# Modulation chunks two slots earlier, the norms in four banks and the first batch's solution ahead of the second's level, in a hybrid delta-rule, state-space and mixture-of-experts layer

## What is computed

```
mod = silu(c) @ w_ada + b_ada            # 6 x 1024 shifts, scales and gates
u   = modulate(x, shift1, scale1) @ w_in  # and the same for the context
q, k, v, xs, b, c = silu(dwconv(u))       # 5 taps along the tokens
k = l2norm(k); q = l2norm(q) / 8          # over 64 channels of each head
M = I + tril(beta k k^T * exp(G_i - G_j)) # per chunk of 64 tokens, head, direction
U = M^-1 (beta v);  W = M^-1 (beta k exp(G))
S = S exp(g_last) + k_dec^T (U - W S)     # chunk after chunk: 4 of the context, 4 of the tokens
o = q exp(G) S + (q k^T * decay) v_new    # two directions, then norm and gate
x = x + g1 * rms_norm(concat(o, ssd) @ w_out)
x = x + g2 * rms_norm(moe(modulate(x, shift2, scale2)))   # 32 experts, 4 per token
```

## Time and profile before

| | |
|---|---|
| median of three timed runs | 1428.35 us (1425.06 to 1429.14) |
| the profiled execution's own time | 1420.88 us |
| its span, first to last instruction | 1419.1 us |
| mean granted TensorE clock | 0.956 |
| TensorE busy | 1255.7 us (88%) |
| VectorE busy | 485.3 us (34%) |
| ScalarE busy | 254.8 us (18%) |
| GpSimd busy | 122.0 us (9%) |

### The profile page before, as it was taken

One profiled execution on the slowest core, in us unless ns is written; L12 is line 12 of the kernel. 1 busy time (PEld: TensorE's weight loads), 2 busy tenths in 40 slices (PEclk: granted clock), 3 DMA queues, 4 the chain that ended last, 5 costly groups with the idle time before them and its releaser, 6 DMA issues.

```text
span 1419.1 us, 25289 instructions
## 1 busy us (share of the span) xinstructions
PE 1255.7 (88%) x10245; PEld 570.7 (40%) x10246; DVE 485.3 (34%) x1026; ACT 254.8 (18%) x494; POOL 122.0 (9%) x169
## 2 busy tenths in 40 slices
PE   5999898547897999999898988987999999999995
PEld 2645354446744333333333333332333333333432
DVE  1255359815767322221222212221222212212223
ACT  2321532325223111111111111110000100100101
POOL 0200370163401000000000000000000000000000
PEclk9999999657997999999999999999999999999998
DMA  9929210000384999999999999999999699969993
GB/s 356 357 88 370 87 55 35 4 33 4 136 297 189 426 425 428 428 426 426 428 427 428 426 426 427 427 426 424 428 427 428 260 426 427 427 265 429 427 427 146
DMA packets 48134, 458.59 MB, mean 323 GB/s; under 512 B 4416, under 2 KB 4816, under 8 KB 22736
## 3 DMA queue, kind: packets, MB, share of 16 engines
q1 hardware_dynamic: 48080, 457.81, 77.8%
HBM read 456.15 MB, written 1.05 MB: 322 GB/s over the span
## 4 chain that ended last, share of the span: by engine, by line
PE 57%; DMA 29%; DVE 6%; issue 3%; ACT 2%; POOL 1%; DVEq 0%; SPq 0%; ACTq 0%; POOLq 0%
DMA arena<-in_w_up 29%; PE bank L1155 22%; PE bank L1184 8%; PE bank L667 7%; PE bank L1126 3%; PE bank L1117 2%; PE bank L1048 2%; PE bank L583 2%; PE bank L543 2%; DVE arena L1727 1%; ACT arena L1542 1%; PE bank L592 1%; DMA arena<-in_x 1%; PE bank L1148 1%; PE bank L897 1%
## 5 line engine op out<-in xcount | busy, mean ns | idle before, releaser
L1155 PE MATMUL bank<-arena 128*64 128x512 f32 x2176 | 482.8, 596 | 35.2 <-DMA arena<-in_w_up 19.5
L1155 PEld LDWEIGHTS bank<-arena 128*64 128x64 f32 x2176 | 154.1, 137 | 345.2 <-issue 269.4
L1184 PE MATMUL bank<-arena 128*64 128x512 f32 x1088 | 239.3, 592 | 0.0
L2254 DVE TENSOR_SCALAR arena<-bank 128x512 f32<-128x512 f32 x34 | 23.6, 693 | 394.0 <-PE bank L1155 394.0
L1184 PEld LDWEIGHTS bank<-arena 128*64 128x64 f32 x1088 | 78.1, 136 | 138.4 <-issue 136.0
L667 PE MATMUL bank<-arena 128*128 128x512 f32 (+1 forms) x320 | 123.8, 541 | 0.0
L2235 DVE TENSOR_TENSOR arena<-arena,bank 128x512 f32<-128x512 f32 x140 | 86.6, 681 | 6.0 <-PE bank L1126 6.0
L667 PEld LDWEIGHTS bank<-arena 128*128 128x128 f32 x320 | 60.7, 194 | 59.6 <-issue 57.0
L1117 PEld LDWEIGHTS bank<-arena 128*128 128x128 bf16 x1680 | 60.3, 118 | 27.0 <-DVE arena L2258 25.8
L1126 PE MATMUL bank<-arena 64*128 64x512 f32 x280 | 69.6, 614 | 0.9 <-ACT arena L1544 0.9
L1544 ACT ACTIVATE arena<-bank 128x512 f32<-128x512 f32 x34 | 20.4, 600 | 253.2 <-PE bank L1184 253.2
(11 more groups left out here) (346 smaller groups left out, 1076.2 us busy)
## 6 DMA issues: line engine op xcount, KB each, us to landing
arena<-in_w_gate SPq DMA_DIRECT2D x64, 2048.0 KB, 20.5
arena<-in_w_up SPq DMA_DIRECT2D x64, 2048.0 KB, 22.1
arena<-in_w_down SPq DMA_DIRECT2D x64, 2048.0 KB, 20.8
arena<-in_w_ada SPq DMA_DIRECT2D x12, 2048.0 KB, 10.4
arena<-in_wfm SPq DMA_DIRECT2D x20, 512.0 KB, 3.4
arena<-in_wz SPq DMA_DIRECT2D x4, 1024.0 KB, 14.6
arena<-in_w_out SPq DMA_DIRECT2D x2, 2048.0 KB, 8.8
arena<-in_x SPq DMA_DIRECT2D x2, 1024.0 KB, 7.5
```

Of the source, the lines that this page charges most:

```text
L1155: last = mm(ps[m][64 * c_:64 * c_ + 64, :], xcT[:, k, :], ring[:, 2 * h_ + m, k % 4, 512 * c_:512 * c_ + 512], start=False, stop=(k == KT ...
L1184: last = mm(ps[2][64 * c_:64 * c_ + 64, :], hidT[:, k % 4, 64 * (k // 4):64 * (k // 4) + 64], ring[:, 4 + h_, k % 4, 512 * c_:512 * c_ + 5 ...
L2254: v.tensor_scalar(hid[:, 0], ps[0][:, :], LIMIT, None, ALU.min).then_inc(*L.mark("a"))
```

## The change

Five edits belong together. The chunks are used in slots 1 to 8 (ADA_AT = 1). The norm sums go round four banks, 2, 6, 4 and 5, so that a sum waits for the Ln four before it; the first two transpositions, which use banks 4 and 5, wait for the last two Ln there. In a slot TensorE does the row and the chunk ahead of the transpositions, and the chunk decays (`spread_last`, and VectorE's copy) come in slot 10. The decays, Gram products and the diagonal chain start one slot earlier (SOLVE_AT = 11), and GpSimd prepares the first four decays ahead of the multiplications of k and q. In the second stage `solved(0)` stands ahead of `level_p(1)`.

```diff
-ADA_AT = 3
-SOLVE_AT = 12
+ADA_AT = 1
+SOLVE_AT = 11
...
                     pe.wait_ge(*L.at("pool", "sq", i))
-                    if i >= 2:
-                        pe.wait_ge(*L.at("act", "ln", i - 2))
-                    bk = ps[(2, 6)[i % 2]]
+                    if i >= 4:
+                        pe.wait_ge(*L.at("act", "ln", i - 4))
+                    bk = ps[(2, 6, 4, 5)[i % 4]]
...
-                if n >= 2:
-                    pe.wait_ge(*L.at("act", "turned", TURNED[n - 2]))
+                pe.wait_ge(*(L.at("act", "turned", TURNED[n - 2]) if n >= 2 else L.at("act", "ln", 6 + n)))
...
                 if i == NKQ + 1:
                     norms()
-                if i > NKQ and i - 1 in TURNED:
-                    turn(i - 1)
-                if NKQ + 3 <= i < NKQ + 7:
-                    turn(i - NKQ - 3)
-                if i == NKQ + 3:
-                    spread_last()
 
                 use = i - ADA_AT + 4
...
                     ada_chunk(use, 3)
+                if i > NKQ and i - 1 in TURNED:
+                    turn(i - 1)
+                if NKQ + 3 <= i < NKQ + 7:
+                    turn(i - NKQ - 3)
+                if i == NKQ + 2:
+                    spread_last()
                 if i == SOLVE_AT:
                     spread_decays(0)
...
             last_level(0)
+            solved(0)
             level_p(1)
-            solved(0)
             level_x(1)
...
-                        bk = ps[(2, 6)[m % 2]]
+                        bk = ps[(2, 6, 4, 5)[m % 4]]
...
-                if i == NKQ + 3:
+                if i == NKQ + 2:
                     dve.wait_ge(*L.at("pe", "eglb"))
...
                 g_.tensor_tensor(norm_of(i), src, src, ALU.mult).then_inc(*L.mark("sq", i))
...
+            pool.wait_ge(*L.at("dve", "Gs"))
+            pool.wait_ge(*L.at("pe", "ada", 11))
+            for G in range(4):
+                steps_of(G)
+                start_decay(G)
             for i in range(NKQ):
...
                 g_.tensor_tensor(dst, dst, norm_of(i), ALU.mult).then_inc(*L.mark("kT", i))
...
-            pool.wait_ge(*L.at("dve", "Gs"))
-            pool.wait_ge(*L.at("pe", "ada", 11))
-            for G in range(4):
-                steps_of(G)
-                start_decay(G)
             pool.wait_ge(*L.at("dve", "row", 11))
```

More of the change, by code:

```diff
@@ L2348, in _ @@
                 g_.tensor_tensor(norm_of(i), src, src, ALU.mult).then_inc(*L.mark("sq", i))
[L2349 to L2354, removed]
             def start_decay(G):
@@ L2375, in _ @@
                 start_decay(G)
+            for i in range(NKQ):
+                kind, j, both = FM[i]
+                dst = {"k": kT, "q": qT}[kind][:, j]
+                pool.wait_ge(*L.at("act", "rn", i))
+                pool.wait_ge(*L.own())
+                g_.tensor_tensor(dst, dst, norm_of(i), ALU.mult).then_inc(*L.mark("kT", i))
             pool.wait_ge(*L.at("dve", "row", 11))
```

## The result

| | before | after |
|---|---|---|
| median of five runs on the same chip | 1425.06 us (1423.50 to 1429.14) | 1414.65 us (1410.48 to 1416.13) |
| ratio, 95% interval | | 0.9928 (0.9903 to 0.9952) |
| the profiled execution's own time | 1420.88 us | 1415.84 us |
| its span | 1419.1 us | 1414.0 us |
| mean granted TensorE clock | 0.956 | 0.954 |

The change makes the kernel faster by 0.72%, some 10.3 us of 1425 (7 to 14 by the interval). 1414.6 was predicted, from a gain of 13.7. So the total agrees better than the gain does: the first median, 1428.35, on which the forecast stood, lay 3.3 us above the one measured beside the changed kernel.

A forecast was written before the change was run, and what follows sets the result against it. The limit was taken to move between TensorE, the norms' hole, VectorE at the slots' end, and TensorE's waits in the second batch's inversion. Gains 5.5 + 8.2 = 13.7 us off 1428.35 gave 1414.6 us, range 1408 to 1423.

The forecast's parts named there:

- Part 3: Second stage: W and U products moved into TensorE's 11.9 us hole ahead of the second level; gain 8.2 us, bounds 5 and 8.5.
- Slots 1 to 9: Chunks two slots earlier put two more row-and-chunk pairs of 2.8 us ahead of slot 9's end, at 152.7 us.
- the rival with late landings: Slots 3 to 8: chunk loads landing in 14.6 us hold TensorE; net 8.5 us slower, 1436.9 us; chance 0.05.
- Slots 10 to 13: Slot 10's pair and slot 11's row are gone, so slot 14 starts 3.8 us earlier.
- The norms: After slot 9: with four banks the eight Ln run back to back in 4.5 us; slot 10's product starts at 163.8.
- Part 2: Diagonal chain from slot 11: inverse at 244.4; TensorE waits for slot 19's pad copy, first level at 248.2, not 253.66.
- Parts 1 and 2: Earlier chunks, four norm banks and earlier diagonal chain: first level 5.5 us earlier, bounds 2.8 and 8.2.
- the rival in which only part 3 works: End of the slots: VectorE's load finds the earlier slots as late as now, the first gain is lost; 1420.2 us; chance 0.12.
- The shared port: Slot 9's convolution: all four VectorE taps meet GpSimd's steps, costing 2.7 us instead of 1.0; 1416.3 us; chance 0.12.
- the taps over 1 us each in slot 9: Sign of being wrong: convolution taps over 1 us in slot 9.
- the first level at 253 again: Sign of being wrong: the first level starts at 253 us again, where near 248 was forecast.
- W and U did not hold the second level: Sign of being wrong: the second level starts after GpSimd's diagonals because the W and U products still run.

The follow-up runs named there:

- e1: The kernel before with only solved(0) moved ahead of level_p(1): ratio 0.9944 (0.9918 to 0.9971) to the kernel before, median 1415.82 us.
- e2: The changed kernel with solved(0) put back behind level_p(1), so the slot edits alone: ratio 0.9999 (0.9974 to 1.0024) to the kernel before, median 1425.80 us.
- e10: The changed kernel with solved(0) put back and slot 19's product ahead of slot 17's transposition: ratio 0.9941 (0.9917 to 0.9965) to the kernel before.
- e3: The changed kernel with five extra 512-wide products between the fourth and fifth norm product: ratio 0.9900 (0.9861 to 0.9939) to the kernel before.
- e4: The changed kernel with GpSimd's key and query multiplications ahead of its first four decay steps again: ratio 0.9930 (0.9900 to 0.9959) to the kernel before.
- e5: The kernel before with the four banks of the norms alone, chunks staying in slots 3 to 10: 1417.6 us in one run, no ratio.

## Why the prediction was right in its total and wrong in a part

- **Part 3** held in size and place. The hole was there, `solved(0)` took 7.14 us in it at a clock of 0.80, where 0.50 was the fear, and the products that use the level start 1.50 us after the level's last product. 8.2 forecast, 8.0 timed (e1).
- **Slots 1 to 9** held. From the cumulation to slot 9's end TensorE is busy 65.72 of 65.72 us, so no chunk came late; the rival with late landings is out. **Slots 10 to 13** held: 35.76 against 35.7.
- **The norms failed** by 2.65 us (14.75 against 12.1) in this execution, and by 1.2 in those of e2 and e10 with the same slots. The step is "the Ln run back to back", 4.5 us, with slot 10's product right behind them. The first Ln came at 163.28, 7.87 us behind slot 9's product, where 7.45 stood with the allowance for GpSimd (contention 1.33 and not 1.0). But from there to slot 10's product it took 6.88 us and not 4.6. The four banks let TensorE do its first four products at once and then sit idle; the last four and the row product were paid at half pace, and I had priced them from full-clock rows, although the slow row at 154.40 stood in the trace of the kernel before. With the clock kept up (e3) the stretch is 12.24 us.
- **Part 2 failed** at its wait. "It waits for the pad copy of slot 19, which stands on ScalarE behind slot 18's Silu": but the copy stood behind slot 19's product. In the changed kernel Silu 18 begins at 247.18 and the pad copy could have followed it at 247.60; it came at 249.89, idle 2.29 us for TensorE. I had taken TensorE's rows only from 247.04 on; two rows earlier stand the wait of 2.94 us for slot 17's Silu and the slow product behind it. VectorE's own chain was sized right: from slot 15's convolution to the inverse 28.2 us were forecast, and it took 28.24 (221.42 to 249.66).
- The two misses add up: 2.65 + 2.29 = 4.9 us, near the 4.7 by which the first level is late (166.0 us behind the cumulation instead of 161.3). VectorE, though, lost only the first of them: forecast 9.2 earlier, seen 6.7.
- **The bounds and the rivals.** Parts 1 and 2 gave 0 us (e2, at most 3.7) or 0.7 (the two traces), below the lower bound set for them, 2.8; their upper bound, 8.2, "if TensorE's wait for the pad copy vanished too", is what e10 reaches (8.4). What happened is nearest the rival in which only part 3 works. Its place was wrong: it put the loss on VectorE's load, and VectorE was early. The shared port took half of that rival's price: the last of GpSimd's eight operations ended at 159.2 (157.80 + 1.38, quoted below), in the middle of the taps. The lock that the Trainium skill describes (SBUF — State Buffer, section "SBUF: two separate sides") agrees with e4 in direction: the taps fall to 3.12 us when GpSimd's steps are elsewhere. The price measured here is 1.33 us.
- Of the signs that were set down for being wrong two came, the taps over 1 us each in slot 9 (four in 4.45) and the first level at 253 again (166.00 behind the cumulation is 252.9 on the clock of the trace before). No chunk held TensorE, and W and U did not hold the second level.
- That 1414.6 was met is in part chance: some 3.3 us less gain than forecast (13.7 less 10.4, the distance of the two medians), from a base 3.3 us lower than the one it was subtracted from.

## What to carry to other kernels

When an engine's work is moved earlier, follow every input of the operation that it feeds back to a wait, including those that now end just before: the one that is second today sets the end tomorrow, and a short in-order queue (here a transposition in front of a product) is worth reordering only once the first is out of the way. Two such edits can each measure nothing and give 8 us together, so an edit that removes a covered wait should be judged with its partner. A burst that is finished early gains less than its waits suggest if the engine then idles and does its next work at the lower clock: the four banks alone gave 1.4 us where Ln back to back would give 4 to 4.5 (e5).

## What was not expected of the hardware

- Waits of 3.7 to 5.1 us between products were followed by work at half pace: after 3.69 us the last four norm products took 3.75 us and the row 1.88 (e5); after 3.71 us slot 19's product took 5.92 us, not 3.6. The price of such a wait is not fixed: after 2.94 us the same product took 4.69 (before), in e4 a wait of 3.69 us was followed by 3.05 for the same four products, and behind 5.10 us the row took 1.91 in the changed kernel and 1.02 in e2. With five extra products in the gap the clock was 1.00 behind it (e3).
- GpSimd pays too: a step took 1.05 us alone, and beside VectorE's taps, on GpSimd's own timeline of the changed kernel, up to 1.55:

```profile
148.67 1.55 POOL L2360 TENSOR_TENSOR arena<-arena 128x512 f32<-128x512 f32 x1 [8.61 <-PE bank L543]
...
157.80 1.38 POOL L2353 TENSOR_TENSOR arena<-arena 128x512 f32<-128x512 f32 x1
```

- The streams of 32 x 32 and 64 x 64 products stop for what the profile calls "issue", with no wait named. TensorE's rows behind such a stop in the first level, before and after:

```profile
257.16 1.60 PE L782 MATMUL bank<-arena 32*32 32x32 f32 x102 [2.00 <-issue]
```

```profile
259.72 1.61 PE L781 MATMUL bank<-arena 32*32 32x32 f32 x102 [2.53 <-issue]
```

  With the next stop, 128 products on (0.69 us before, 1.24 after), this makes most of the 1.1 us by which the stretch between the two levels grew. The stops hang on the place in the program: they lie 128 products apart, or a multiple of that, and in e3, where TensorE's program has ten more products ahead of them, they come ten products earlier (behind product 141 and not 151 of the second level). What stops the stream there was not tried.
- The first 87 to 93 us vary between executions of the same work by more than most steps of this change are worth (0.96 granted clock at 86.9 us, 0.92 at 89.7). Two profiled spans don't measure a change of 10 us; cuts at a common event do.
